# Forgetting attention in a fused two-block kernel: first two query blocks of a head as one stretch of 384 columns, and three places of other work per pair of heads with a whole slab between

## The reference

```python
def forgetting_attention(q, k, v, f_pre, q_g, k_g):
    q = jnp.moveaxis(rms_norm_2(q, q_g), 1, 2)
    k = jnp.moveaxis(rms_norm_2(k, k_g), 1, 2)
    ...
    F = jnp.moveaxis(jnp.cumsum(jax.nn.log_sigmoid(f_pre.astype(f32)), axis=1), 1, 2)
    ...
        logits = jnp.einsum('bhqd,bhkd->bhqk', q_blk, k).astype(f32) * scale + (F_blk[..., :, None] - F[..., None, :])
        logits = jnp.where(k_pos[None, :] <= q_pos[:, None], logits, -jnp.inf)
        p = jax.nn.softmax(logits, axis=-1)
        return jnp.einsum('bhqk,bhkd->bhqd', p.astype(v.dtype), v)
```

## Time and profile before

| | |
|---|---|
| time, median of 3 runs | 1979.48 us (1979.2 to 1979.71) |
| profiled execution: its own time, its span | 1979.13 us, 1977.3 us |
| PE busy | 1965.5 us (99%) |
| DVE, ACT, POOL busy | 854.6, 771.4, 610.5 us |
| the chain that ended last | matmuls of line 430, 40% of the span |
| granted TensorE clock | 1.000 |

### The profile page before, as it was taken

How to read it: one execution, slowest core, us unless ns; L and a number is a source line. 1 busy time by engine, 2 the same in 40 slices (tenths; PEclk the granted TensorE clock), 3 DMA queues, 4 the chain that set the end, 5 groups by cost and what they waited for, 6 DMA issues and landing times. The chain is left out here.

```text
span 1977.3 us, 27474 instructions
## 1 busy us (share of the span) xinstructions
PE 1965.5 (99%) x9500; PEld 1581.9 (80%) x9500; DVE 854.6 (43%) x1337; ACT 771.4 (39%) x1199; POOL 610.5 (31%) x241
## 2 busy tenths in 40 slices
PE   9999999999999999999999999999999999999999
PEld 7777878888888888888878877777788888888887
DVE  6888663332224434342284445555221363222200
ACT  7444442222223322332266566666422343322211
POOL 0000124444432344444313330000344423444443
PEclk9999999999999999999999999999999999999999
DMA  4111245543332555552212222112233323333322
GB/s 167 54 54 54 78 147 200 191 149 99 102 102 78 191 192 191 195 181 96 90 57 83 74 75 61 58 53 64 65 98 95 103 76 100 102 95 95 109 90 98
DMA packets 56644, 210.76 MB, mean 107 GB/s; under 512 B 6288, under 2 KB 7056, under 8 KB 56592
## 3 DMA queue, kind: packets, MB, share of 16 engines
q1 hardware_dynamic: 56592, 210.08, 32.7%
HBM read 207.96 MB, written 2.10 MB: 106 GB/s over the span
## 5 line engine op out<-in xcount | busy, mean ns | idle before, releaser
L382 POOL TENSOR_TENSOR wlo<-raw,whi 128x1024 fp32r<-128x1024 f32 (+1 forms) x234 | 602.8, 2576 | 1277.8 <-ACT whi L912 1277.8
L430 PE MATMUL bank<-xh,whi 128*128 128x512 f32 x1688 | 668.3, 396 | 2.9 <-DVE qz L1956 1.4
L430 PE MATMUL bank<-xh,wlo 128*128 128x512 f32 x1688 | 657.9, 390 | 0.0
L430 PE MATMUL bank<-xl,whi 128*128 128x512 f32 x1688 | 657.4, 389 | 0.0
L912 ACT ACTIVATE whi<-raw 128x1024 fp32r<-128x1024 f32 (+1 forms) x298 | 330.6, 1109 | 618.6 <-PE bank L430 606.1
L430 PEld LDWEIGHTS bank<-xh,whi 128*128 128x128 f32 x1688 | 317.0, 188 | 82.7 <-issue 13.6
L430 PEld LDWEIGHTS bank<-xh,wlo 128*128 128x128 f32 x1688 | 316.8, 188 | 66.8
L430 PEld LDWEIGHTS bank<-xl,whi 128*128 128x128 f32 x1688 | 317.2, 188 | 64.3 <-issue 1.0
L430 PE MATMUL bank<-acth,whi 128*128 128x512 f32 x528 | 205.6, 389 | 0.3 <-POOL wlo L382 0.3
L430 PE MATMUL bank<-acth,wlo 128*128 128x512 f32 x528 | 205.4, 389 | 0.0
L430 PE MATMUL bank<-actl,whi 128*128 128x512 f32 x528 | 205.4, 389 | 0.0
(11 more groups left out here) (322 smaller groups left out, 1916.1 us busy)
## 6 DMA issues: line engine op xcount, KB each, us to landing
raw<-w_dram SPq DMA_DIRECT2D x250, 512.0 KB, 3.6
adaw<-ada_dram SPq DMA_DIRECT2D x72, 512.0 KB, 4.3
raw<-wd_dram SPq DMA_DIRECT2D x48, 704.0 KB, 4.1
h<-x_dram SPq DMA_DIRECT2D x4, 512.0 KB, 6.5
out_dram<-h SPq DMA_DIRECT2D x8, 256.0 KB, 3.5
rel<-rel_dram SPq DMA_DIRECT2D x1, 513.0 KB, 5.9
crow<-c_dram SPq DMA_DIRECT2D x1, 512.0 KB, 3.6
gates_raw<-gates_dram SPq DMA_DIRECT2D x1, 384.0 KB, 5.3
```

What stands on the lines that cost most here:

```text
L382: nc.gpsimd.tensor_tensor(wlo[:, s, 0:width], raw[:, s, 0:width], whi[:, s, 0:width].bitcast(F32), ALU.subtract).then_inc(sem("w_lo"), 1)
L430: mm = nc.tensor.matmul(proj[b][:], w[:, s, W], v[:, k, :], start=first and j == 0 and a == 0, stop=last and j == len(chunks) - 1 and a == ...
```

## The change

The first two query blocks share bank 2 + e: block 0 has columns 0 to 128, block 1 columns 128 to 384 (`block_at`). Their scores, maxima, exponentials, divisions and turns are done one after the other for both blocks, in the order k = 0, 2, 1, 3 (`SHORT`). One ACT copy per head takes all 384 columns to `fpT` (`fox_copy_two`) instead of one of 128 and one of 256. The scores of blocks 0 and 1 of pair t + 1 stand in the last place of pair t.

That leaves three places per pair. Between them stands always a whole slab: slab `s` behind the turns of blocks 0 and 1 and the scores of block 2, slab `s + 1` behind the turns of block 2 and the scores of block 3, slab `s + 2` behind the turns of block 3. On ACT `split` of slab `s + 1` moves behind the exponentials of block 2; on DVE `weight_low` moves likewise. The last pair gets chunks by a new `LAST_BESIDE`: 7, then 1 and 5, then 3.

```diff
-        BESIDE = (((0, 0, 6),), ((0, 6, 8), (1, 0, 5)), ((1, 5, 8), (2, 0, 3)), ((2, 3, 8),))
-        LAST_BESIDE = (((1, 0, 5),), ((1, 5, 8), (2, 0, 2)), ((2, 2, 6),), ((2, 6, 8),))
+        LAST_BESIDE = {1: ((1, 0, 7),), 2: ((1, 7, 8), (2, 0, 5)), 3: ((2, 5, 8),)}
+        SHORT = (0, 2, 1, 3)
+        def place(k):
+            return k if k > 3 else SHORT.index(k)
+        def block_at(b):
+            return slice(P, 3 * P) if b == 1 else slice(0, (b + 1) * P)
...
             def fox_scores(t, tt, b, beside=lambda: None):
-                pe.wait_ge(sem("probs"), t * 8 + (UA + 2 * b))
+                pe.wait_ge(sem("probs"), t * 8 + (UA + (2 * b if b > 1 else 0)))
...
@@ fox_pair of PE
-                for b in range(NB):
-                    fox_turn(t, 2 * b)
-                    fox_turn(t, 2 * b + 1)
-                    if b == 0:
+                for b in range(1, NB):
+                    for k in SHORT if b == 1 else (2 * b, 2 * b + 1):
+                        fox_turn(t, k)
+                    if b == 1:
                         fox_turn_values(t, i, s - 2)
-                        fox_scores(t, tt, 1)
-                    elif b + 1 < NB:
-                        if more and b == 2:
+                        fox_scores(t, tt, 2)
+                    elif b == 2:
+                        if more:
                             fox_squares(i, s)
-                        fox_scores(t, tt, b + 1, beside=lambda: fox_values(t, b - 1))
+                        fox_scores(t, tt, 3, beside=lambda: (fox_values(t, 0), fox_values(t, 1)))
+                        if more:
+                            fox_sums(s)
                     else:
-                        fox_values(t, NB - 2)
+                        fox_values(t, 2)
                         if more:
                             fox_scores(t + 1, 1 - tt, 0)
...
+                            fox_scores(t + 1, 1 - tt, 1)
+                    if more:
+                        if b == 3:
+                            pe.wait_ge(sem("f_ln"), t * 2 + 3)
+                        wide("fox", i, 6, s + b - 1)
+                        continue
...
@@ before the loop, PE
             fox_scores(0, 0, 0)
+            fox_scores(0, 0, 1)
             wide("fox", 0, 6, 3, part=(4, KC))
...
+            def fox_copy_two(t, e):
+                act.wait_ge(sem("pT_ready"), t * 8 + (UA + 2 * e + 2))
+                act.wait_ge(sem("values"), t * 8 + UA)
+                nc.scalar.activation(fpT[:, e, 0:3 * P], bank[5 + e][:, 0:3 * P], ACT.Copy).then_inc(sem("pT_copied"), 2)
...
@@ fox_pair of ACT, new body up to the copies of block 2
+                if more:
+                    fox_tile(t + 1, i, s - 1, 0, later=True)
+                else:
+                    merge_tile(0)
+                for k in (4, 5):
+                    fox_exps(t, k)
+                if more:
+                    split(i, 6, SLAB["fox"], s + 1, WC)
+                    fox_tile(t + 1, i, s, 1)
+                else:
+                    merge_tile(1)
+                for k in (4, 5):
+                    fox_copy(t, k)
...
@@ before the loop, DVE (fox_pair of DVE: the same order)
-            for k in range(2):
+            for k in SHORT:
                 fox_maxima(0, k)
             weight_low(0, 6, SLAB["fox"], 4)
-            for k in range(2):
+            for k in SHORT:
                 fox_scale(0, k)
```

More of the change, by code:

```diff
@@ L113, in build @@
         gates_raw = sb("gates_raw", [P, KC * 96])
-        stat = sb("stat", [P, 2, 8])
+        stat = sb("stat", [P, 4, 8])
         lg = sb("lg", [P, 2 * RH])
@@ L792, in fox_scores @@
                     H = slice(e * DH, e * DH + DH)
-                    nc.tensor.matmul(bank[2 + e][:, 0:W], fq[H, tt, b * P:W], fk[H, tt, 0:W], start=True, stop=False,
+                    nc.tensor.matmul(bank[2 + e][:, C], fq[H, tt, b * P:W], fk[H, tt, 0:W], start=True, stop=False,
                                      skip_group_check=True)
@@ L796, in fox_scores @@
                     H = slice(e * DH, e * DH + DH)
-                    nc.tensor.matmul(bank[2 + e][:, 0:W], selp[H, tt, :], fsp[H, 0:W], start=False, stop=False,
+                    nc.tensor.matmul(bank[2 + e][:, C], selp[H, tt, :], fsp[H, 0:W], start=False, stop=False,
                                      skip_group_check=True)
@@ L800, in fox_scores @@
                 for e in range(2):
-                    nc.tensor.matmul(bank[2 + e][:, W - P:W], identb[:], leb[:], start=False, stop=True,
+                    nc.tensor.matmul(bank[2 + e][:, C.stop - P:C.stop], identb[:], leb[:], start=False, stop=True,
                                      skip_group_check=True).then_inc(sem("scores"), 1)
@@ L1354, in merge_tile @@
                                          bias=c1("b_merge", j // 2)).then_inc(sem("evac0"), 1)
-                if j > 0:
-                    split(0, 4, SLAB["merge"], j + 2, WC)
+                split(0, 4, SLAB["merge"], j + 2, WC)
             def fox_pair(i, tt, more=True):
@@ L1361, in fox_pair @@
                 s = 3 * tt + 4
[L1362 to L1382, removed]
@@ L1383, in fox_pair @@
-                if more:
-                    fox_exps(t + 1, 0)
-                    fox_exps(t + 1, 1)
+                for e in range(2):
+                    fox_copy_two(t, e)
+                act.wait_ge(sem("f_vT"), t + 1)
+                nc.scalar.activation(fv[:].rearrange("p b n -> p (b n)"), bank[4][:], ACT.Copy).then_inc(sem("f_v"), 1)
+                if more:
+                    fox_tile(t + 1, i, s - 1, 0, later=True)
[3 more added lines that the diff above has]
+                    fox_exps(t, k)
@@ new lines, in fox_pair @@
+                if more:
[5 more added lines that the diff above has]
+                    fox_copy(t, k)
+                fox_exps(t, 6)
+                if more:
+                    fox_log(t + 1, s, 1)
+                fox_exps(t, 7)
+                if more:
+                    fox_log(t + 1, s, 0)
+                    fox_root(t + 1, 1)
+                    fox_root(t + 1, 0)
+                    split(i, 6, SLAB["fox"], s + 3, WC)
+                    fox_values(i, s + 1)
@@ L1386, in fox_pair @@
+                for k in (6, 7):
+                    fox_copy(t, k)
+                if more:
+                    for k in SHORT:
+                        fox_exps(t + 1, k)
+                else:
+                    merge_tile(2)
                 act.wait_ge(sem("values"), t * 8 + (UA + 8))
                 nc.scalar.activation(chunk(ybh, t), bank[7][:], ACT.Copy).then_inc(sem("yb_hi"), 1)
-                if more:
-                    split(i, 6, SLAB["fox"], s + 4, WC)
             for j in (1, 0):
@@ L2075, in fox_pair @@
                 s = SLAB["fox"] + 3 * tt + 4
[L2076 to L2087, removed]
+                for k in (4, 5):
+                    fox_maxima(t, k)
+                for k in (4, 5):
+                    fox_scale(t, k)
+                if more:
+                    weight_low(i, 6, s, 1)
+                    fox_selector(t + 1, 1 - tt)
+                for k in (6, 7):
+                    fox_maxima(t, k)
+                if more:
+                    weight_low(i, 6, s, 2)
+                for k in (6, 7):
+                    fox_scale(t, k)
                 if more:
@@ L2091, in fox_pair @@
                     weight_low(i, 6, s, 3)
[L2092 to L2095, removed]
+                    for k in SHORT:
+                        fox_maxima(t + 1, k)
+                    for k in SHORT:
+                        fox_scale(t + 1, k)
                 dve.wait_ge(sem("yb_hi"), t + 1)
```

55 lines of the change are left out of this document (28 added, 27 removed).

## The result

The changed kernel takes 1998.15 us (median of 6 runs, 1998.0 to 1998.53); the kernel before, run beside it on the same chip, 1979.49 us (1979.2 to 1980.12). The ratio is 1.0094, with a 95% interval of 1.0084 to 1.0105: slower by 18.7 us, where +12.4 us was forecast, and outside the range by 1.65 us. The sign and the mechanism in the stage of the pairs were as forecast, and a third of the loss is somewhere else.

The account below looks back on a forecast made before the run. PE, busy 99% of the span, was taken to bound the kernel; -1.8 + 11.5 + 1.7 + 1.0 = +12.4 us on the profiled 1979.13 us gave 1991.5 us, 0.6% slower, range 1986 to 1996.5 us.

Parts of the forecast that it names:

- The wait for the keys: Behind block 2's turns PE waits in `fox_squares` for ACT's evacuation of slab `s`: 1.64 us in seven pairs, +11.5 us.
- no wait: Rival at the key tile: the evacuation is covered, no change that can be told, 1980.4 us; 4 in 100.
- half a wait: Rival at the key tile: PE waits only 0.8 to 1.2 us per pair, total 1984 to 1988 us; 9 in 100.
- a second wait per pair: Rival: block 3's turns or `f_qk` also come 0.5 to 1 us late in seven pairs, 1995 to 1999 us; 8 in 100.
- The clock stayed at 1.00: Rival, PE in the pairs: waiting drops the clock to 1.2 GHz for one slab in seven pairs, 2030 us; 3 in 100.
- The first pair: Ahead of the first pair, DVE's longer chain of maxima and divisions delays the turns: +1.7 us, bounds 1.0 and 2.3.
- The last pair: In the last pair, five chunks ahead of block 3's turns do not cover the chain: +1.0 us, between 0 and 2.
- The division beside POOL that was kept for the upper bound: In the last pair, the first head's division overlaps POOL's work on merge slab 3: up to 0.4 us more, once.
- The edges: On PE, one return to a slab less and values grouped together save 0.23 us per pair, 8 pairs: -1.8 us.
- The twelve values in one go: On PE, values of blocks 0 and 1 together take 0.81 us instead of 0.96, saving 0.15 us per pair.
- The sum of the stage: All terms, in the stage of the pairs: -1.8 + 11.5 + 1.7 + 1.0 = +12.4 us.
- PE's busy sum should stay near 1965 us, since no work is added: Sign for the profile after, whole kernel: PE's busy time stays near 1965 us, as no matmul is added or removed.

Follow-up runs that it names:

- experiment 5: Changed kernel with `stat` as 4 rows of 4, reciprocal in column 3, every tensor at its old place; 1992.33 us, ratio 1.0067 to the kernel before.
- Experiment 4: Changed kernel with `stat` of 6 rows and the wait for the keys moved between the values of blocks 0 and 1; 1995.81 us, ratio 1.0081.
- experiment 1: Kernel before with only `stat` enlarged to 4 rows of 8, all behind it moved by 64 bytes; 1985.61 us, ratio 1.0029.
- experiment 2: Kernel before with only `stat` enlarged to 6 rows of 8, all behind it moved by 128 bytes; 1993.2 us, ratio 1.0068.
- experiment 7: Kernel before with a pad of 128 unused bytes ahead of all tensors, so everything moves together; 1979.25 us, ratio 0.9999.
- experiment 8: Kernel before with a pad of 128 unused bytes ahead of `acth`, moving `acth` and `actl` alone; 1988.51 us, ratio 1.0045.
- experiment 9: Kernel before with 128 unused bytes between `xl` and `raw`, moving the weights and all behind them but not `xh` and `xl`; 2004.56 us, ratio 1.0125.

## Why the prediction was right in the stage and wrong in sum

Against its own steps; the distances are the same in the changed kernel and, within a few hundredths of a us, in the kernel with the old places (experiment 5):

- **The wait for the keys** was forecast at 1.64 us seven times, 11.5 us. By PE's starts it costs 11.9 us, 1.7 us each: ACT began 0.53 us behind the slab's last matmul instead of 0.49, and PE went on 0.10 us behind the evacuation instead of 0.05. Experiment 4 takes it away and gets 10.1 us back, most of the rest being the price of a wait between the values. The rivals of no wait, half a wait and a second wait per pair are refuted by the same list: seven waits of 1.6 us, and none of L822 in the loop. (The half wait's own sum was slightly off: seven times 0.8 to 1.2 us with the other terms is 1986 to 1988 us, not 1984 to 1988.) The clock stayed at 1.00.
- **The first pair**, +1.7 us, measures 1.7 us by starts, partly as a wait and partly as stretched turns.
- **The last pair**, +1.0 us, measures 1.1 us. The division beside POOL that was kept for the upper bound came about: 1.08 us against 0.48.
- **The edges**, -1.8 us, were forecast as 0.23 us per pair and measure 0.23 us. The twelve values in one go came out at the 0.81 us expected.
- **The sum of the stage** is +12.67 us between the slab starts around it, against +12.4. The four terms as measured add up to 12.9 us (11.9 + 1.7 + 1.1 - 1.8); where the 0.2 us between the two lie is open.

**The step that failed** is the one behind "PE's busy sum should stay near 1965 us, since no work is added", and behind a sum that has terms for the stage alone. The number of matmuls stayed, and their length did not. PE's busy sum rose by 5.3 us, and the whole of the missing 5.9 us (18.7 - 12.8) comes from 64 bytes more in `stat`. The prediction gives that hunk no term and no reason for leaving it out. The rows of before could not have given its size: there no moving operand stands badly, and the large groups all read 389 to 396 ns. But it is an edit that reaches every later projection, and it should have been named as one whose price no row bounds. Experiments 1, 2 and 5 show that the place of the tensors costs it, and 7 to 9 that what counts is the distance between the moving operand and the tensors among which the weights stand; that it is the weights themselves rests on the argument under experiment 9. That experiment 1 by itself has 6.0 us and the changed kernel 5.9 us on the same shift closes the account. How the distance acts is open.

## What to carry to other kernels

Where PE is busy all the time, a reordering on it can only win at its edges, here 0.23 us per pair. It loses wherever a reader is moved up to a slab's end: the evacuation was done 2.7 us behind the start of the slab's last matmul here, and all of that which no other work covers is lost. Count for each wait what stands between the last matmul and it. A larger tensor in the list of allocations moves all behind it; when a change makes matmuls longer that it doesn't touch, compare the mean row by operand, and put sizes back to what they were before judging the change. Keep a moving operand and its weights at a distance that has been measured to be good (here those of the kernel before, and 256 bytes more for what stands behind `stat`), since the wrong one cost 0.3 to 1.3% of the whole kernel.

## What was not expected of the hardware

A matmul of 512 float32 columns with weights loaded beside it takes 0.227 us from start to start, or up to 0.233 us, by where its moving operand lies relative to the weights and their neighbours. In the kernel before `xh` and `acth` lie a multiple of 256 bytes from `whi` and from `wlo` (44032 and 38656 bytes from `whi`, by the program's allocation). A shift by 256 bytes costs nothing, by 64, 128 or 192 it costs 6.0, 13.6 or 15.4 us over the matmuls that stream from behind `stat`, and with the weights moved by 128 bytes against `xh` and `xl` 25.0 us. Moving both by 128 bytes costs nothing (experiment 7).

The distance modulo 256 is not the whole of it. At 128 bytes all three matmuls of a chunk in the down projections are slower (395 ns each in experiment 2). At 64 bytes the two that stream `acth` are (392 and 393 ns in experiment 1), and the one that streams `actl` is not (389 ns, as before), though `acth` and `actl` lie 45056 bytes apart, a multiple of 256, and both were shifted by the same 64 bytes. In the window from 1890 to 1960 us three matmuls take 0.687 us there, 0.680 us before and 0.700 us in experiment 2.

The weights are loaded while an earlier matmul runs (in the changed kernel the load for the matmul of 1233.58 starts at 1233.35, beside the matmul that starts then), so I take the two reads to meet in some part of the memory that repeats every 256 bytes. This is argued and not shown, and it doesn't say why `actl` is spared at 64 bytes. The Trainium skill (TensorE: Matmul & The Clock Gate, Part 2) has TensorE read the two through independent ports, and says that loading the next tile's weights takes no read bandwidth from the running matmul. By that rule the distance would not matter; experiments 8 and 9 measure that it does, and the measurement decides. Open is also whether 256 bytes is the period itself or a multiple of it, why 192 bytes costs more than 64, and whether other widths or types show it.
